# Two decoder blocks on one core: the first projections on unscaled, host-turned features, the root behind them, the gate chain five tiles later

## What is computed

```
hn = rmsnorm(h, ln_mix_w)                      # x * root * w, root = rsqrt(mean(x*x) + eps), one per token
proj = hn @ w_in
q, k, v, g_out, g_low, z, xbc, dt_raw, ... = split_cols(proj, IN_SPLITS)
log_g = log_sigmoid(g_low @ gla_w_gate2 + gla_b_gate) / 16
o = gla_chunked(q * 128**-0.5, k, v, log_g)
o = rmsnorm(o, gla_norm_w) * silu(g_out)
...
dt = softplus(dt_raw + dt_bias);  a = dt * (-exp(a_log))
```

## Time and profile before

| | us |
|---|---|
| median of 3 runs | 1517.35 (1517.27 to 1517.61) |
| profiled execution, its own time | 1515.03 |
| its span in the trace | 1513.2 |
| TensorE busy | 1363.6 (90%) |
| VectorE busy | 1049.1 (69%) |
| ScalarE busy | 676.5 (45%) |

### The profile page before, as it was taken

How to read it: one execution, slowest core, us unless ns; L and a number is a source line. 1 busy time by engine, 2 the same in 40 slices (tenths; PEclk the granted TensorE clock), 3 DMA queues, 4 the chain that set the end, 5 groups by cost and what they waited for, 6 DMA issues and landing times.

```text
span 1513.2 us, 17803 instructions
## 1 busy us (share of the span) xinstructions
PE 1363.6 (90%) x6585; PEld 982.7 (65%) x6585; DVE 1049.1 (69%) x2081; ACT 676.5 (45%) x1226; POOL 303.0 (20%) x265
## 2 busy tenths in 40 slices
PE   6999999999999888787877777878899999999997
PEld 6989999879896333233323333333398788998876
DVE  5767688776698777777677677665786465765554
ACT  5665876556464222221222222222454465645662
POOL 1000000000025554454444444442100000000000
PEclk9999999999999998999899998999999999999999
DMA  7454655445879999999999999999765556555542
GB/s 245 153 172 131 198 166 155 140 140 178 304 300 385 421 422 421 421 421 421 422 421 421 421 422 422 421 421 421 292 207 176 148 178 189 163 173 145 161 143 80
DMA packets 78054, 417.65 MB, mean 276 GB/s; under 512 B 8768, under 2 KB 8832, under 8 KB 44944
## 3 DMA queue, kind: packets, MB, share of 16 engines
q0 software_dynamic: 36864, 268.45, 42.8%
q1 hardware_dynamic: 41104, 148.06, 31.0%
HBM read 415.39 MB, written 1.08 MB: 275 GB/s over the span
## 4 chain that ended last, share of the span: by engine, by line
PE 55%; DMA 28%; DVE 10%; ACT 4%; issue 1%; POOL 1%; DVEq 0%; POOLq 0%; ACTq 0%
DMA AR<-in_peer_uv,C 16%; PE ps L1045 14%; PE ps L1047 13%; PE ps L1046 13%; DMA SLAB<-in_peer_uv,C 12%; PE ps L1332 7%; DVE wlo L1920 2%; DVE AR L2237 1%; DVE SLAB L2237 1%; PE ps L1266 1%; ACT whi L1498 1%; POOL SLAB L2470 0%; ACT AR L1708 0%; POOL AR L2470 0%; PE ps L1251 0%
## 5 line engine op out<-in xcount | busy, mean ns | idle before, releaser
L1920 DVE TENSOR_TENSOR wlo<-raw,whi 128x1024 fp32r<-128x1024 f32 x246 | 299.3, 1221 | 163.6 <-ACT whi L1498 163.0
L1332 PE MATMUL ps<-SLAB,AR 128*128 128x512 f32 x520 | 261.2, 654 | 67.6 <-ACT AR L1708 66.2
L1498 ACT ACTIVATE whi<-raw 128x1024 fp32r<-128x1024 f32 x246 | 258.6, 1056 | 128.9 <-PE ps L1047 116.8
L1045 PE MATMUL ps<-XH,whi 128*128 128x256 f32 (+1 forms) x1032 | 300.0, 291 | 1.9 <-DVE XL L2153 1.2
L1047 PE MATMUL ps<-XH,wlo 128*128 128x256 f32 (+1 forms) x1032 | 293.3, 284 | 0.0
L1332 PE MATMUL ps<-AR 128*128 128x512 f32 x504 | 241.7, 629 | 57.2 <-ACT AR L1708 55.3
L1046 PE MATMUL ps<-XL,whi 128*128 128x256 f32 (+1 forms) x1032 | 293.2, 284 | 0.0
L2470 POOL DMA_INDIRECT AR<-in_peer_uv,C x126 | 144.6, 1148 | 583.3 <-DVE C L1900 420.0
L1332 PEld LDWEIGHTS ps<-SLAB,AR 128*128 128x128 f32 x520 | 106.2, 209 | 216.8 <-issue 123.4
L1332 PEld LDWEIGHTS ps<-AR 128*128 128x128 f32 x504 | 98.8, 201 | 197.4 <-issue 113.3
L2237 DVE CUSTOM_DVE_ANT_0 SLAB<-SLAB,AR 128x1024 f32<-128x1024 f32 x130 | 158.3, 1223 | 74.1 <-DMA SLAB<-in_peer_uv,C 74.0
(11 more groups left out here) (374 smaller groups left out, 1462.2 us busy)
## 6 DMA issues: line engine op xcount, KB each, us to landing
raw<-in_stream SPq DMA_DIRECT2D x246, 512.0 KB, 4.1
AR<-in_stream SPq DMA_DIRECT2D x9, 512.0 KB, 8.1
AR<-scr SPq DMA_DIRECT2D x8, 512.0 KB, 5.7
SLAB<-in_peer_uv,C POOLq DMA_INDIRECT x130, 28.4
AR<-in_rows SPq DMA_DIRECT2D x4, 512.0 KB, 5.5
AR<-in_peer_uv,C POOLq DMA_INDIRECT x126, 28.2
AR<-in_con SPq DMA_DIRECT2D x1, 1280.0 KB, 7.3
AR<-in_xin SPq DMA_DIRECT2D x2, 512.0 KB, 4.2
```

Of the source, the lines that this page charges most:

```text
L1045: pe.matmul(o, sh, mh, start=first, stop=False)
L1332: t = pe.matmul(ps[2 * i + half][:, :], d, rows_in[:, 512 * half:512 * half + 512], start=c == 0, stop=c == 127)
L1498: a.activation(in_two(whi[i % NS][:, :]), src, ACT.Copy).then_inc(*hi.up(i))
L1920: v.tensor_tensor(in_two(wlo[i % NS][:, :]), src, in_two(whi[i % NS][:, :]).bitcast(F32), ALU.subtract).then_inc(*lo.up(i))
```

## The change

The host now also hands in the features turned, xt: 8 columns of ln_mix_w and then eight pieces of 272 tokens (feature-major). These are loaded in two halves behind tile 0. ScalarE and VectorE make high and low halves XH0 and XL0 of the unscaled features times the gain (step raw_x), and tiles 0 to 24 (small, k, q, v, g) run on them. Tile 0 takes its products as the pieces arrive; in tiles 1 to 3 the products with wlo stand last. TensorE runs 11 matmuls on ones ahead of tile 0. The squares and the root (step x_roots) come behind the splits of tiles 0 to 4 in the queues of ScalarE and VectorE, and x, the meta tokens and the constants behind tiles 0 to 3 in SyncE's.

After tile 4 the root is spread over the partitions by three products of ones with diagonals into RBX, and SMT is multiplied by it (step small). In tiles 5 to 14 the eight feature pieces are scaled by RBX in place (scaled_x, VectorE) and split anew (high_x on ScalarE, low_x on VectorE) for the state space part. k, q and v stay unscaled until the root comes in elsewhere: the silu of g takes it as its scale, the token-major v takes its square, and eps of the attention's norm is scaled to match.

gates_side is registered after tile 9 (v0) in place of tile 4, and in the g stream two of its steps are taken a tile. The core of the diff:

```diff
     yield say("begin")
-    for c in range(5):
-        if c < 4:
-            yield say("scale", c)
...
+    yield from split(0)
+    for k in range(8):
+        yield say("raw_x", k)
+    for i in range(1, 5):
+        yield from split(i)
+    yield say("x_roots")
...
         if c == "k3":
+            yield say("spread_x")
+            yield say("small")
+        n = i - RESCALED_FROM
+        for k, part in ((n - 2, "low_x"), (n - 1, "high_x"), (n, "scaled_x")):
+            if 0 <= k < 8:
+                yield say(part, k)
+        if c == "v0":
             side(gates_side())
...
+    at["steps"] = 2
     yield from stream_N("g", 2, 8, plain("g"))
+    at["steps"] = 1
...
+                if step == "begin":
+                    on.wait_ge(*dve.of("ones"))
+                    for _ in range(WARMING):
+                        pe.matmul(ps[5][:, 0:128], ONES, ONES, start=True, stop=True)
...
                 elif step == "gate_sums":
-                    on.wait_ge(*act.of("small"))
+                    on.wait_ge(*dve.of("small"))
+                    on.wait_ge(s_par, 32)
...
-                    a.activation(SG[:, tt, blk * 512:blk * 512 + 512], ps[b][:, :], ACT.Silu).then_inc(*act.up(("g", blk, tt)))
+                    a.activation(SG[:, tt, blk * 512:blk * 512 + 512], ps[b][:, :], ACT.Silu, scale=ss[:, tt:tt + 1]).then_inc(*act.up(("g", blk, tt)))
...
+                elif step == "scaled_x":
+                    k, = at
+                    on.wait_ge(*dve.of(("raw_x", k)))
+                    on.wait_ge(*act.of("spread_x"))
+                    v.tensor_tensor(XTK[:, k, :], XTK[:, k, :], RBX, ALU.mult).then_inc(*dve.up(("scaled_x", k)))
...
+                    load(0)
+                    sp.dma_start(XT[:, 0:half], xt[:, 0:half]).then_inc(s_xt[0], 16)
+                    sp.dma_start(XT[:, half:8 + 8 * T], xt[:, half:8 + 8 * T]).then_inc(s_xt[1], 16)
+                    for n in range(1, NR):
+                        load(n)
                     sp.dma_start(HX[:, 0, :], x_tiles[:, 0, :]).then_inc(s_x0, 16)
```

More of the change, by code:

```diff
@@ L28 @@
 LAST_WIDE = 240
+WARMING = 11
 NEG = -3.0e38
@@ L860, in order_of_work, with build @@
     yield say("sb_post")
-def build(nc, stream, par, rows, con1, con2, xin, meta, subk, peer_uv, out):
+def build(nc, stream, par, rows, con1, con2, xin, xt, meta, subk, peer_uv, out):
     ctx = ExitStack()
@@ L900, in build @@
         HX = place("hx", 0, 3072).rearrange("p (i d) -> p i d", i=3)
+        XT = place("xt", 11208, 8 + 8 * T)
+        XTK = XT[:, 8:8 + 8 * T].rearrange("p (k t) -> p k t", k=8)
+        XH0, XL0 = ARR[:, 17872:17872 + 8 * T], ARR[:, 17872 + 8 * T:17872 + 16 * T]
+        RBX = place("rbx", 8480, T)
+        RD = place("rd", 13400, 16 + 256)
+        ONES = place("ones", 13672, 128)
         x_tiles = xin.rearrange("(i p) d -> p i d", p=128)
@@ L1078, in tensor_program @@
             for step, *at in order_of_work():
[L1079 to L1087, removed]
-                    pe.transpose(ps[b][:, 16:144], HX[:, 0, f], ident)
-                    pe.transpose(ps[b][:, 144:272], HX[:, 1, f], ident).then_inc(*side.up(("turn_x", k)))
-                    free[b] = dve.of(("turn_x", k))
+                if step == "begin":
+                    on.wait_ge(*dve.of("ones"))
+                    for _ in range(WARMING):
+                        pe.matmul(ps[5][:, 0:128], ONES, ONES, start=True, stop=True)
+                elif step == "spread_x":
+                    on.wait_ge(*dve.of("x_diagonals"))
+                    pe.matmul(ps[4][:, 0:16], ONES[0:16, :], RD[0:16, 0:16], start=True, stop=True)
+                    for i in range(2):
+                        m = pe.matmul(ps[4][:, 16 + 128 * i:144 + 128 * i], ONES, RD[:, 16 + 128 * i:144 + 128 * i], start=True, stop=True)
+                    m.then_inc(*side.up("spread_x"))
+                    free[4] = act.of("spread_x")
                 elif step == "T":
@@ L1095, in tensor_program @@
                     ws = slice(k % 8 * 128, k % 8 * 128 + 128)
+                    if i == 0:
+                        o, by = ps[b][:, 0:n], lambda j: slice(128 * j, 128 * j + 128)
+                        on.wait_ge(*act.of(("raw_x", k)))
+                        pe.matmul(o, whi[0][:, by(k)], xh, start=k == 0, stop=False)
+                        on.wait_ge(*lo.of(0))
+                        pe.matmul(o, wlo[0][:, by(k)], xh, start=False, stop=False)
+                        for j in (k - 2,) if k < 7 else (5, 6, 7):
+                            if j >= 0:
+                                _, low, ready = moving[what](j, t0, n)
+                                on.wait_ge(*ready)
+                                m = pe.matmul(o, whi[0][:, by(j)], low, start=False, stop=j == 7)
+                        if ends:
+                            m.then_inc(*prod.up((i, 1)))
+                        continue
+                    if i < 4:
+                        o = ps[b][:, 0:n]
+                        if k == 0:
+                            on.wait_ge(*hi.of(i))
+                            bank(b)
+                        pe.matmul(o, whi[i][:, ws], xh, start=k == 0, stop=False)
+                        pe.matmul(o, whi[i][:, ws], xl, start=False, stop=False)
+                        if ends:
+                            on.wait_ge(*lo.of(i))
+                            for j in range(8):
+                                m = pe.matmul(o, wlo[i][:, 128 * j:128 * j + 128], moving[what](j, t0, n)[0], start=False, stop=j == 7)
+                            m.then_inc(*prod.up((i, 1)))
+                        continue
                     if k % 8 == 0:
@@ L2443, in pool_program @@
             for step, *at in order_of_work():
[L2444 to L2452 removed]
+                if step == "gather":
                     m, j, before = at
@@ L2620, in lay_params, with lay_features @@
     return p
+def lay_features(inp):
+    both = np.concatenate([np.asarray(inp["meta_tokens"]), np.asarray(inp["x"])[0]], axis=0)
+    turned = both.T.reshape(8, 128, T).transpose(1, 0, 2).reshape(128, 8 * T)
+    return np.concatenate([columns(inp["ln_mix_w"]), turned], axis=1)
 def lay_rows(inp):
```

129 lines of the change are left out of this document (70 added, 59 removed).

## The result

| | before | after |
|---|---|---|
| median of 9 runs each, taken together | 1517.00 us (1515.6 to 1517.61) | 1521.06 us (1520.29 to 1521.80) |
| ratio after / before | | 1.0028 [1.0020, 1.0036] |
| profiled execution | 1515.03 us | 1520.92 us |
| its span | 1513.2 us | 1519.1 us |

The changed kernel is slower by 4.1 us, 0.28%. The forecast was 1519.6 us, in a range from 1513.0 to 1523.0. By the forecast's own chances "within 0.2% of before" was the likeliest outcome (0.51); what came is the slower one (0.36). The medians differ by 4.1 us, the two profiled executions by 5.9: that of after is near its median, that of before 2.0 us under its own. So of a difference between the two traces up to 2 us belong to the execution and not to the kernel.

The account below looks back on a forecast made before the run. TensorE's stream of weight tiles was taken to bound the kernel before, with VectorE's gate chain without slack. Tile 23 at +0.1 us and clock +2.2 made +2.3 on 1517.35: 1519.6 us, range 1513.0 to 1523.0.

Parts of the forecast that it names:

- The start: TensorE up to tile 5: first product at 6.5 us, tile 5 at 22.95 instead of 34.15.
- Tile 4's low half is ready at 17.7 ... It just fits: Before tile 5: root at 20.7, tile 5's low half at 22.8, just before TensorE needs it at 22.95.
- slower, by the root: Rival at the start: tile 4 landing at 17.5 instead of 15.4 delays the chain, losing 2 us, 1521.6; 30%.
- Tile 5 later than 24: Sign at the start: tile 5, expected near 23, starting after 24 us would show the forecast wrong.
- The chain: VectorE's queue from the gate sums to decay_row: 47.4 us, from 38.3 to 85.7.
- The wait: TensorE in the middle of tile 22: waits some 7.0 us for decay_row, from 78.75 to 85.75.
- The two small waits: TensorE before decay: tile 18 waits 0.3 us and tile 19 2.0 us for their low halves.
- The clock: TensorE behind the decay_row wait: half clock costs 1.7 to 2.7 us, taken as 2.2.
- zero at the lower end if the wait is under 3 us: Behind the decay_row wait: clock cost can be zero if that wait is under 3 us.
- Nothing is started earlier: Rival at the start: features land late, tile 0 starts as before, later chain costs 9 us more, 1528; 3%.
- The chain is shorter or the clock holds: Rival at decay_row: VectorE ends 3 us earlier, wait 4 us, no clock fall, 1514.5; 14%.
- the lead is kept: Rival at decay: TensorE waits for nothing there, 1510.5, only if VectorE's 47.4 us were under 41; 6%.

Follow-up runs that it names:

- before_v0: Kernel before, with only the gate chain registered after tile 9 and two side steps a tile in the g stream; 1526.29 us, ratio 1.0073.
- gates_q0: Changed kernel with the gate chain registered after tile 5 instead of tile 9 and one side step a tile in the g stream; 1513.01 us, ratio 0.9976.
- roots_first: Changed kernel with the root's squares and the root ahead of tile 4's split in the queues of ScalarE and VectorE; 1519.9 us, ratio 1.0026.
- warm_fill: Changed kernel plus 26 unused matmuls of ones just ahead of TensorE's wait on decay_row; 1518.75 us, ratio 1.0013.
- roots_q0: gates_q0 with the edit of roots_first added; 1513.96 us, ratio 0.9985.
- gates_q0_late: gates_q0 with the scaled feature pieces starting at tile 7 instead of tile 5; 1512.56 us, ratio 0.9972.
- short_chain: Changed kernel without the last four of the seven polynomial steps of dt on VectorE, so its output is wrong; 1516.18 us in one run.
- no_warm: Changed kernel without the eleven matmuls of ones ahead of tile 0; 1520.49 us in one run.
- v0_one_step: Changed kernel with one side step a tile in the g stream instead of two, decay product in the middle of tile 26; 1515.54 us, ratio 0.9993.
- roots_q0_late: roots_q0 with the scaled feature pieces starting at tile 7 instead of tile 5; 1512.38 us, ratio 0.9976.

## Why the prediction held

**What bounds, and the one mechanism.** That the early start would be eaten by the gate chain, with one wait on decay_row, was right. before_v0 and gates_q0 show it from both sides: the moved chain with two steps a tile gives the wait and 11 us of loss without the early start, and the early start with the chain at tile 5 gives a gain. The sizes, by the steps of the sum:

| step | predicted | measured |
|---|---|---|
| first product | 6.5 | 6.47 |
| tile 5 | 22.95 | 25.05 (+2.1) |
| gate products to the end | 39.55 | 41.60 (+2.05) |
| chain on VectorE | 47.4 | 48.7 (+1.3) |
| wait on decay_row | 7.0 | 6.02 |
| decay product to tile 23, clock included | 4.2 | 3.8 (-0.4) |
| tile 23 | 90.0 | 92.99 (+3.0) |

The three errors make up the error of tile 23: 2.1 and 1.3 less 0.4 are 3.0. The prediction had tile 23 behind that of before by 2.3 us, the trace has it behind by 5.3.

**The start was put too early by 2.1 us**, the largest miss. Tile 1 starts at 10.64 (+0.34), tiles 1 to 3 take 0.2 more, tile 4 waits 1.13 for the bank, and from tile 4 to tile 5 it is 3.96 where tile and spread were put at 3.54 (+0.4). The step that failed is "Tile 4's low half is ready at 17.7 ... It just fits": I checked tile 4's data and the root, but not the bank, whose copy stands behind both in ScalarE's queue. By the sum's own times this copy comes after 20.7, while tile 4 was to start at 19.4. roots_first shows it by moving the copy up to 17.44. Over the six executions with this start the miss at tile 5 is 1.0 to 2.6 us.

It is not the rival "slower, by the root", though the range that this rival brought in covers it. Tile 4's transfer did come later than predicted (ScalarE takes it up at 16.48, 1.1 behind the 15.4), at half the size that the rival named, and the root's last step on VectorE ends at 21.5 where the sum had 20.7; but the spread of the root stands directly behind tile 4 (24.27) and waits for nothing. The sum also puts 512 KB at 420 GB/s at 1.28 us, where they are 1.25. "Tile 5 later than 24" was given as a sign that the forecast would be wrong; it was later, and that the time still fell into the range is luck in part: the range had been drawn up to 1523.0 for a late root with 3.4 us of delay, and another delay of this size came.

**The chain was too short by 1.3 us.** A feature piece takes 0.41 to 0.47 us, not 0.36 (one is from the row at 43.26 to the row at 43.67 below), and the eight of them 3.5 us, where 2.8 were summed. And where two polynomial steps follow each other without a low half, as two steps a tile bring it, the second is 0.78 behind the first (76.32 to 77.10), where the sum gave a step 0.67 (1.81 less a low half of 1.14):

```profile
43.26 0.50 DVE L1989 SCALAR_TENSOR_TENSOR XL<-AR,XH 128x272 fp32r<-128x272 f32 x1
43.67 0.44 DVE L1984 TENSOR_TENSOR AR<-AR 128x272 f32<-128x272 f32 x1
...
76.32 0.42 DVE L2045 TENSOR_TENSOR AR<-AR 32x272 f32<-32x272 f32 x1
77.10 0.43 DVE L2045 TENSOR_TENSOR AR<-AR 32x272 f32<-32x272 f32 x1
```

The waits for ScalarE came nearly as summed: 3.89 for the softplus, where the sum has 3.75 (43.2 to 46.95), and 3.13 before the low half at 58.10, the same as in the earlier trace rows. before_v0, whose chain has no pieces, takes 45.9, which is 2.8 less: the pieces' 3.5 less 0.5 that its longer wait for the softplus (4.37) takes back are 3.0.

**The wait** was predicted at 7.0 and is 6.0, since the first half of tile 22 was done 4.4 us late (83.15 against 78.75; 2.05 of it from the start and 1.6 of slow clock behind tile 19's wait, which the sum did not have) and the chain only 3.4. The two small waits before it were put at 0.3 and 2.0 and are 0.76 and 1.83. The wait's end counts, not its length: TensorE's own delays ahead of it cost nothing. That is why I don't count the slow clock behind tile 19's wait as a loss of the changed kernel, though the trace has it.

**The clock** was priced at 2.2 between 1.7 and 2.7; warm_fill gives 1.7 and the comparison with before 1.8 (3.82 less 2.03). The mechanism and the lower bound were right. But "zero at the lower end if the wait is under 3 us" was wrong: the clock fell behind 2.96 us and, in some executions, even behind 1.83.

The Trainium skill ("TensorE: Matmul & The Clock Gate", Part 1: The HAM clock gate) says that an idle array falls back to half clock, and its table prices this at half of the time spent there. The trace comes near it: 3.82 us at 0.50 against 2.12 at 1.00 are 1.70, where half of 3.82 would be 1.9, an estimate by that page's rule.

**The other rivals.** "Nothing is started earlier" gave 1528, 10.7 us over before, for a moved chain without an early start. before_v0 is nearly this kernel, without the feature pieces, and 10.4 to 11.1 us over before: the mechanism was priced well, only the start did come earlier. "The chain is shorter or the clock holds" and "the lead is kept" did not happen either; the chain was longer. From 1519.6 to the measured 1521.06 the miss is 1.5 us in the medians, 3.6 in the profiled executions (1517.3 predicted, 1520.92 measured). The first is within what differs from run to run of one kernel here, and so it flatters the sum: the error of the mechanism is the 3.0 us at tile 23, and half of it vanishes in the medians because the profiled execution of before is a short one.

## What to carry to other kernels

When a change starts a stream earlier, follow the slowest side chain from its own start to the instruction that waits for it, and not only the bounding engine: the lead is worth what this chain lets through. A chain that starts five tiles later (some 15 us of tiles) while its consumer comes half a tile earlier cost 9.4 us at tile 23 of before_v0; in the changed kernel with its consumer 66 products later the loss against before was gone. So when the start of a chain moves, look at where the instruction stands that waits for it. For each moved step, ask also for the buffer that the next tile writes, and for what stands ahead of its release in an in-order queue. A lead read at one place must be read again further down, since it may be work put off.

## What the hardware showed that I had not expected

**The clock fell behind waits of under 2 us, and not in every execution.** The same wait of 1.8 to 1.95 us before one tile is in all of these kernels. In two of them, by windows, first gates_q0 and then roots_q0:

```profile
60.10:64.10 4.00, 4.00 (x22) 4.00 (x23) 3.83 (x9) 1.74 (x3) 0.00 (x0) 0.65 0.44 131
```

```profile
61.50:65.00 3.50, 3.29 (x24) 3.07 (x24) 3.33 (x8) 1.74 (x3) 0.00 (x0) 1.00 0.53 150
```

Both follow an idle time of 1.94 or 1.95 us; the first is granted 0.65, the second 1.00. Of ten profiled executions with such a wait, one of each kernel, the clock fell behind it in six: after (0.63 from 71.5 to 76), gates_q0, gates_q0_late, roots_first, short_chain and no_warm. It held in warm_fill, v0_one_step, roots_q0 and roots_q0_late. In after, seven products of 512 columns, from the row below to 75.53, were each 0.43 us ahead of the next where 0.23 is the rule; with the two gaps at the edges it is 1.6 us:

```profile
72.97 0.63 PE L1063 MATMUL ps<-whi,ARR 128*128 128x512 f32 x1
```

In after this is covered by the wait on decay_row. In gates_q0, where nothing waits behind it, it isn't: some 15 products of 272 columns, from 61.21 to 64.74, are 0.23 apart instead of 0.125 there: 1.5 us, the term of clock in the 7.0 above. And it fell without such a wait: in the three kernels with the slow tile 6, TensorE had idled 0.57, 1.28 and, in gates_q0_late, only some 0.15 us before the gate products, which are eight short records with 16 rows over 2.1 us; gates_q0 had the same gate products without a wait, and its clock held. What decides whether the clock falls was not tried, and one profiled execution of each kernel can't tell a cause from chance. A kernel with such a wait should be counted with 0 to 1.7 us of clock behind it.
